# Three stages of a hybrid layer become one: gates, triangular solve and scans, with two pieces of linear attention moved in the order of TensorE

## The reference

```python
# gated delta rule, 4 heads, keys and values of 128
diff = G[..., :, None] - G[..., None, :]                 # G: running sum of the log decay
decay = jnp.where(causal, jnp.exp(jnp.where(causal, diff, 0.0)), 0.0)
lower = jnp.eye(c) + jnp.where(strict, einsum(k_beta, k) * decay, 0.0)
uw = triangular_solve(lower, concatenate([v * beta, k_beta * exp(G)]))
attn = einsum(q, k) * decay
def step(S, chunk):                                       # scan over the chunks
    v_new = u - w @ S
    o = (q * exp(g)) @ S + attn @ v_new
    S = S * exp(g_last) + (k * exp(g_last - g)).T @ v_new
# gated linear attention, 4 heads, keys of 64, values of 128
def step(S, chunk):
    o = (q * exp(b)) @ S + attn @ v
    S = diag(exp(b_last)) @ S + (k * exp(b_last - b)).T @ v
```

## Time and profile before

| what | value |
|---|---|
| median of 3 runs | 2036.91 us (2035.85 to 2037.27) |
| the profiled execution | 2038.26 us, of which 2036.6 us lie between its first and last instruction |
| mean granted TensorE clock | 0.984 |
| PE busy | 1942.1 us, 95% |
| DVE busy | 1173.8 us, 58% |
| ACT busy | 850.5 us, 42% |
| POOL busy | 338.9 us, 17% |

### The profile page before, as it was taken

How to read it: one execution, slowest core, us unless ns; L and a number is a source line. 1 busy time by engine, 2 the same in 40 slices (tenths; PEclk the granted TensorE clock), 3 DMA queues, 4 the chain that set the end, 5 groups by cost and what they waited for, 6 DMA issues and landing times. The chain is left out here.

```text
span 2036.6 us, 26346 instructions
## 1 busy us (share of the span) xinstructions
PE 1942.1 (95%) x10678; PEld 1561.7 (77%) x10678; DVE 1173.8 (58%) x1459; ACT 850.5 (42%) x1212; POOL 338.9 (17%) x276
## 2 busy tenths in 40 slices
PE   8999898999989899898999999999999999999998
PEld 5887876788887688555788888878789878888886
DVE  4655866565676632476577357545654467736752
ACT  4246533435733522464444234333344445413432
POOL 1500614230151400242220000012000021000002
PEclk9999999999989899999999999999999999999999
DMA  6220121222012132201132333224222112232221
GB/s 242 83 74 31 44 84 62 104 83 83 1 44 104 62 104 99 77 1 44 62 122 70 106 104 104 80 96 145 83 83 83 42 42 104 84 113 88 99 85 70
DMA packets 30780, 167.60 MB, mean 82 GB/s; under 512 B 2827, under 2 KB 9635, under 8 KB 14916
## 3 DMA queue, kind: packets, MB, share of 16 engines
q1 hardware_dynamic: 30228, 165.13, 23.4%
q10 hardware_dynamic: 432, 0.79, 0.1%
HBM read 159.58 MB, written 10.00 MB: 83 GB/s over the span
## 5 line engine op out<-in xcount | busy, mean ns | idle before, releaser
L318 PE MATMUL psum<-inputs_high,weights_high 128*128 128x512 f32 x928 | 382.2, 412 | 20.3 <-DVE inputs_low L266 11.9
L319 PE MATMUL psum<-inputs_low,weights_high 128*128 128x512 f32 x928 | 365.0, 393 | 0.0
L320 PE MATMUL psum<-inputs_high,weights_low 128*128 128x512 f32 x928 | 364.5, 393 | 0.0
L2215 PE MATMUL psum<-inputs_high,weights_high 128*128 128x512 f32 x704 | 276.1, 392 | 0.5 <-DVE inputs_low L2359 0.5
L2216 PE MATMUL psum<-inputs_low,weights_high 128*128 128x512 f32 x704 | 274.0, 389 | 0.0
L2217 PE MATMUL psum<-inputs_high,weights_low 128*128 128x512 f32 x704 | 274.0, 389 | 0.0
L271 DVE TENSOR_TENSOR weights_low<-weights_raw,weights_high 128x2048 fp32r<-128x2048 f32 x66 | 155.4, 2355 | 165.3 <-ACT weights_high L260 165.3
L318 PEld LDWEIGHTS psum<-inputs_high,weights_high 128*128 128x128 f32 x928 | 176.5, 190 | 74.8 <-DVE inputs_low L266 14.2
L319 PEld LDWEIGHTS psum<-inputs_low,weights_high 128*128 128x128 f32 x928 | 176.5, 190 | 38.9 <-issue 5.7
L320 PEld LDWEIGHTS psum<-inputs_high,weights_low 128*128 128x128 f32 x928 | 176.0, 190 | 37.9
L2195 ACT CAST weights_high<-weights_raw 128x2048 fp32r<-128x2048 f32 (+1 forms) x72 | 119.5, 1660 | 166.4 <-PE psum L2217 166.4
(11 more groups left out here) (404 smaller groups left out, 3130.2 us busy)
## 6 DMA issues: line engine op xcount, KB each, us to landing
weights_raw<-w_stream SPq DMA_DIRECT2D x116, 1024.0 KB, 4.9
weights_raw<-w_down SPq DMA_DIRECT2D x32, 704.0 KB, 4.1
residual_parked<-residual SPq DMA_DIRECT2D x2, 2048.0 KB, 9.8
residual_back<-residual_parked SPq DMA_DIRECT2D x2, 2048.0 KB, 8.4
residual<-x_t SPq DMA_DIRECT2D x2, 1024.0 KB, 9.8
bias_by_row<-bias_rows SPq DMA_DIRECT2D x2, 1024.0 KB
bias_by_row<-bias_rows SPq DMA_DIRECT2D x1, 1536.0 KB
out_t<-residual SPq DMA_DIRECT2D x5, 256.0 KB, 2.0
```

Of the source, the lines that this page charges most:

```text
L318: pe.matmul(out, hi, self.ahi[:, k], start=start and b == 0, stop=False)
L319: pe.matmul(out, hi, self.alo[:, k], start=False, stop=False)
L320: mm = pe.matmul(out, lo, self.ahi[:, k], start=False, stop=stop and b == blocks - 1)
L2215: pe.matmul(out, wh, hi, start=start, stop=False)
```

## The change

`delta_gates`, `solve` and `scans` no longer make a block each. They return their engines' parts as functions, and a new `recurrences` runs all of them in one block with one set of 41 semaphores, so that each engine goes from one stage to the next when its own waits allow. Waits are added where the block's end had stood: PE's `zero_left` and `turned_read`, ACT's `pair_read` before it clears four banks, DVE's and SP's `scaled`, and PE's wait for the first finished chunk of the last level before the scans. `cleared` keeps ACT from reading a transfer's semaphore before SP has cleared it. SP's two loads of weights (1 MB each) go out once the gates have read the buffer. ACT's part of the weight split moves from the first scan step to the end of the solve.

Linear attention's products of the first chunk (`gla_adds(0)` and both halves of `gla_outputs(0)`, 16 instructions) move from the scans' first step into the solve's first level, on PE between `left` of chunk 1 and of chunk 2. In the scans `gla_adds(1)` and `gla_adds(2)` run one step earlier than before, and the second half of `gla_outputs(t)` runs one step later, between `carried` and `solved`. DVE's wait at the end of a step goes, and one for `gla_out` comes in front of the second half of the state update. The banks of `carried` and `solved`, and the two sets of banks of linear attention, change places.

```diff
+def recurrences(nc, k, layer, h, a, gla, squares):
+    with ExitStack() as stack, phase(nc, "cleared", "row", ..., "gla_early") as s:
+        gates = delta_gates(nc, k, h, a, s, stack)
+        scan = scans(nc, k, h, a, gla, squares, s, stack)
+        inverse = solve(nc, k, layer, h, a, s, scan.linear)
+        with nc.Block() as block:
...
+            @block.tensor
+            def _(pe):
+                gates.tensor(pe)
+                inverse.tensor(pe)
+                scan.tensor(pe)
...
 # solve
+    def sync(sp):
+        sp.sem_inc(s.cleared, 1)
+        sp.wait_ge(s.scaled, 3 * HEADS)
+        sp.wait_ge(s.pair, TT)
         for u in range(2):
             sp.dma_start(k.raw[:, u], ...).then_inc(k.landed[u], 16)
...
         def left(n, t):
+            if n == 0 and t < COUPLED:
+                pe.wait_ge(s.coupled, t + 1)
             if n < mid and 4 * n + t >= COUPLED:
...
+        pe.wait_ge(s.zero_left, 1)
+        pe.wait_ge(s.turned_read, 2 * HEADS)
         for t in range(TT):
             left(0, t)
+            if t == COUPLED - 1:
+                linear(pe)
...
     # scalar, at its end
+        act.wait_ge(s.cleared, 1)
+        act.wait_ge(k.landed[0], 16)
+        act.copy(k.whi[:, 0], k.raw[:, 0]).then_inc(s.high, 1)
...
     # vector, at its start
+        dve.wait_ge(s.scaled, 3 * HEADS)
...
     # gpsimd
                 if n:
                     pool.wait_ge(s.left, 4 * (n - 1) + t + 1)
                     pool.wait_ge(s.inv_t, t + 1)
+                else:
+                    pool.wait_ge(s.pair_read, t + 1)
 # scans
+    def linear(pe):
+        gla_adds(pe, 0)
+        gla_outputs(pe, 0, (0, 1), False)
+        gla_outputs(pe, 0, (2, 3), True)
     def tensor(pe):
+        pe.wait_ge(s.inv_t, TT * (len(LEVELS) - 1) + 1)
         for t in range(TT):
...
                 mm.then_inc(s.carried, 1)
-                if t < end:
-                    gla_adds(t)
+                if t == 1:
+                    pe.wait_ge(s.gla_state, 2)
+                    gla_adds(pe, 2)
+                else:
+                    if t > 2:
+                        pe.wait_ge(s.gla_state, 2 + HEADS * (t - 2))
+                    gla_outputs(pe, t - 1, (2, 3), True)
                 pe.wait_ge(s.rest, t)
...
             mm.then_inc(s.solved, 1)
             if t == 0:
-                gla_adds(t)
+                gla_adds(pe, 1)
             else:
                 pe.wait_ge(s.gla_state, max(2, HEADS * (t - 1)))
-            if t >= 2:
-                pe.wait_ge(s.gla_out_copy, t - 1)
-            gla_outputs(t, (0, 1), False)
+                if t >= 2:
+                    pe.wait_ge(s.gla_out_copy, t - 1)
+                gla_outputs(pe, t, (0, 1), False)
             pe.wait_ge(s.values, t + 1)
...
             mm.then_inc(s.out, 1)
-            if t > 1:
-                pe.wait_ge(s.gla_state, 2 + HEADS * (t - 1))
-            gla_outputs(t, (2, 3), True)
+        pe.wait_ge(s.gla_state, 2 + HEADS * (end - 1))
+        gla_outputs(pe, end, (2, 3), True)
     def vector(dve):
...
             if t > 1:
+                dve.wait_ge(s.gla_out, t)
                 gla_state(t - 1, (2, 3))
...
-            dve.wait_ge(s.gla_out, t + 1)
         rest(end)
+        dve.wait_ge(s.gla_out, end)
         gla_state(end - 1, (2, 3))
```

More of the change, by code:

```diff
@@ L946, in delta_gates @@
     q, kk, v = h.qkv[:, 0:4], h.qkv[:, 4:8], h.qkv[:, 8:12]
[L947 to L1051, removed]
-                row(2)
-                row(3)
-                for n in range(4, 2 * HEADS, 2):
-                    row(n)
-                    row(n + 1)
-                    turn(n // 2)
-                for n in range(HEADS, HEADS + 2):
-                    turn(n)
-                pe.wait_ge(s.kb, HEADS)
-                for n in range(2 * TT):
-                    cols = slice((n % TT) * P, (n % TT + 1) * P)
-                    if n >= 2:
-                        pe.wait_ge(s.pair_read, n - 1)
-                    for hd in range(HEADS):
-                        mm = pe.matmul(ps[:, n % 2, hd * P:(hd + 1) * P], kk[:, hd, cols],
-                                       (kb if n < TT else q)[:, hd, cols], start=True, stop=True)
-                    mm.then_inc(s.pair, 1)
-                    if n in (1, 3):
-                        turn(HEADS + 2 + n // 2)
@@ L1076, in solve @@
+    return named(scalar=scalar, vector=vector, gpsimd=gpsimd, tensor=tensor)
+def solve(nc, k, layer, h, a, s, linear):
     ps, con = k.ps, k.con
@@ new lines, in recurrences @@
+def recurrences(nc, k, layer, h, a, gla, squares):
+    with ExitStack() as stack, phase(
+            nc, "cleared", "row", "row_exp", "diff", "decay", "masked", "kb", "scaled", "turned", "turned_read",
+            "last_arg", "last_exp", "pair", "pair_read", "coupled", "zero_left",
+            "coupling", "left", "left_copy", "both", "inv", "inv_t", "zero_both",
+            "zero", "carried", "rest", "solved", "values", "out", "out_copy", "added", "state", "gla_out", "gla_out_copy",
+            "gla_added", "gla_state", "squared", "high", "split", "gated", "gla_early") as s:
+        gates = delta_gates(nc, k, h, a, s, stack)
+        scan = scans(nc, k, h, a, gla, squares, s, stack)
+        inverse = solve(nc, k, layer, h, a, s, scan.linear)
@@ L1173, in _ @@
-                for t in range(TT):
-                    left(0, t)
-                for m in range(first_step, steps + behind):
-                    if m < steps:
-                        left(m // TT, m % TT)
-                    if m - behind >= first_step:
-                        both((m - behind) // TT, (m - behind) % TT)
+                gates.tensor(pe)
+                inverse.tensor(pe)
+                scan.tensor(pe)
+            @block.vector
+            def _(dve):
+                gates.vector(dve)
+                inverse.vector(dve)
+                scan.vector(dve)
@@ L1233, in _ @@
+                gates.scalar(act)
+                inverse.scalar(act)
+                scan.scalar(act)
             @block.gpsimd
             def _(pool):
[L1235 to L1241 removed]
@@ L1400, in gate_outputs @@
+                gates.gpsimd(pool)
+                inverse.gpsimd(pool)
+                scan.gpsimd(pool)
 def gate_outputs(dve, s, k, h, t, mixers, copied=None):
```

620 lines of the change are left out of this document (365 added, 255 removed).

## The result

The changed kernel takes 2023.5 us in the median (2022.07 to 2026.19, 4 runs) against 2037.09 (2035.85 to 2039.1, 4 runs): a ratio of 0.9935 with a 95% interval of 0.9923 to 0.9947. That is 13.6 us faster, where 6.7 were forecast, and lies outside the range. The profiled execution takes 2023.1 us, of which 2021.3 lie in the span; the span before was 2036.6, so 15.3 us are to be explained.

The account below looks back on a forecast made before the run. POOL's masks were taken to set the solve's pace, PE the scans'. The terms 0.39 + 0.9 + 0.85 + 0.32 + 0.9 give 3.36 us a layer, 6.7 for two: 2030.2 against 2036.91, range 2027 to 2034.

Parts of the forecast that it names:

- Gates to solve: Without the block's end POOL's masks of the solve start earlier and all 18 move: 0.39 us saved a layer.
- Linear attention in the first level: The 16 instructions moved into the solve's first level take 1.79 us on PE, hidden by POOL's masks: no cost.
- Rival 1: Those 16 instructions run at low clock, POOL waits 1.75 us a layer: 2033.7 us, no change; chance 0.09.
- Solve to scans: PE goes from the solve's last products to `solved` of step 0 without the block end's wait: 0.9 us saved a layer.
- first step: Scans' step 0: PE issues 32 instructions instead of 40 between `solved` and `carried`, clock returning as before: 0.85 us saved a layer.
- The bound of 3.5 us: Upper bound of the saving in the scans' step 0, if none of the 32 instructions runs at low clock.
- Step 1: Scans: half of `gla_outputs(1)`, 0.90 us on PE, leaves, but DVE's weight split limits the saving to 0.32 us a layer.
- step 2: Scans: nothing follows `out`, so `carried` of step 3 comes 0.9 us earlier a layer; DVE fits by 0.3.
- Rival 3: DVE becomes the bound of the scans' step 2 as well, 0.9 us a layer lost: 2032.0 us; chance 0.11.
- step 3: Scans: half of `gla_outputs(2)`, 0.9 us, fills the 0.85 in which PE waited for DVE; no change in length.
- SP's later transfer: At the next stage's start SP clears 41 semaphores instead of 19; its first transfer comes 1.2 us later, hidden.
- Rivals 2 and 4: Scans' low clock: returns some 5.3 us later, 2035.5 us, chance 0.08; or stays through the whole scans, 2068, chance 0.03.

Follow-up runs that it names:

- cut_gates: The changed kernel with the block end between gates and solve put back, solve and scans still in one block; 2030.0 us.
- spread: The changed kernel with linear attention's 16 instructions moved from the solve's first level, two into each of the solve's last eight steps; 2027.8 us.
- before_filled: The kernel before with two idle instructions, whose result nobody reads, added in each of the solve's last eight steps; 2034.4 us.
- after: The changed kernel itself, in its first measurement and profile; 2023.5 us against 2037.09 for the kernel before.
- again: The changed kernel, unaltered, measured and profiled once more; 2025.9 us.
- split_early: The changed kernel with DVE's first weight split moved to its idle time at the solve's end, and the clearing of `gst` given to GpSimd; 2024.5 us.
- late_half: The changed kernel with DVE's weight split early, `gst` cleared on GpSimd, and eight of linear attention's 16 instructions in the solve's last steps; 2027.4 us.
- after_later: The changed kernel with DVE's subtraction before the last solved step of the second layer's scans made three times instead of once; 2029.4 us.

## Why the prediction was right in its order and wrong in its time

- **Gates to solve, 0.39.** Right: 0.40 and 0.55 up to the last mask. `cut_gates`, with the block end back, shows 38.55 and 38.66 there.
- **Linear attention in the first level, nothing.** Right: the 16 instructions start 0.112 apart, and POOL shows no idle time. Without POOL's cover they cost 16.11 - 14.20 = 1.9 (`spread` against the first layer of the changed kernel, both at the high clock), near the 1.79 worked out. Rival 1 is out.
- **Solve to scans, 0.9; first step, 0.85.** Right at one clock: 0.85 and 0.77. Wrong in the profile, where both together gave 4.90 and 2.74. The step that failed is the sentence that the clock "comes back as long after the start as before". It stayed up in one layer and came back some 3.3 us after `solved` in the other (588.53 to 591.8), where 4.2 to 5.4 were taken over; so `carried` of step 1 came 3.77 and 5.28 after `solved`, where 6.25 was forecast. The bound of 3.5 us stood in the text for the first step alone, and I placed myself in its middle from two measured ramps that both had the block end in them. For the solve's end the sum priced no change of the clock at all.
- **Step 1, 0.32; step 2, 0.9.** Right: `solved` of step 2 comes 268.71 - 259.76 = 8.95 after `carried` of step 1, where it was 9.25, and `carried` of step 3 comes 4.62 behind it instead of 5.5. DVE's split did become what PE waits for. Rival 3 is out; step 3 changed by 0.06.
- **SP's later transfer.** Right: it is issued 2.3 us after the next stage's first cast, and nothing waits for it.
- **What no term held.** Order and waits come to 0.40 + 0.55 + 2 x (1.61 + 1.19 + 0.06) = 6.7 us, the sum that was forecast. The rest of the 15.3, 8.6 us, is the clock: 4.90 + 2.74 - 2 x 1.61 = 4.4 at the solve's end, and 4.2 in stages that the change doesn't touch. The sum has no term for the stages behind the second layer, and that is the second step that failed. Rivals 2 and 4 looked for a longer low stretch; a shorter one was in the text only as the first step's bound, and no chance was given to it by itself. That order and waits come so near to the forecast sum is no luck, since its terms hold one by one; the time as a whole missed. Single runs agree, as far as the mean granted clock of a run tells: two of the kernel before had 0.989 and took 2031.6 and 2033.3, and four of the changed kernel with 0.989 took 2025.7 to 2027.9, some 6 us less, where the medians lie 11.3 to 13.6 apart.

Shown: filling the solve's end removes the low stretch there, and the block end before the scans goes with a longer one. Why it does is not shown; the rows suggest that the standstill in the low stretch puts off the return of the clock. A standstill of 0.78 us did not bring the clock down by itself: in both layers of `before_filled` it happens at 1.00 and the clock stays. The Trainium skill, TensorE: Matmul & The Clock Gate, section "HAM oscillation — how this bites in real kernels", tells of waits for transfers between groups of products that bring the low clock back. Those waits are longer than 0.78 us, so `before_filled` neither bears that out nor speaks against it.

Not settled: why the later stages take 1405.7 to 1406.4 us in four of the sixteen profiles (after, again, split_early, cut_gates) and 1408.7 to 1410.3 in the other twelve. The clock goes with it: up to the span's end these stages spend 19.8 to 23.0 us at the low clock in the four, 28.4 to 35.9 in the twelve. All four have the new order. The place goes with it too: the first low stretch behind the second layer begins 61.5 to 62.1 us after the next stage's first cast in the four and 59.6 to 60.4 in eleven of the twelve (`late_half`, at 1408.7, has 61.6). With its delay `after_later` went from the first place to the second; the kernel before, delayed, only reached 60.4, so whether the place gives the fast form was not tested. So 4.2 of the 15.3 us in the profile may be lost again to any edit that shifts these stages.

## What to carry to other kernels

Work out the saving at one clock, and then ask separately whether the stretch begins or ends at the low clock, what would lengthen or shorten that, and how much work lies under it: here this second sum was larger than the first. A block end in a stretch at the low clock may cost more than its idle time: here such stretches were 3.4 us longer. Before a gain is credited to an edit, look at the stages that it doesn't touch, and repeat the profile: one execution shows only one of several places where the clock may fall.

## What the runs showed of the hardware that was not expected

The same code at the same place shows low stretches of different length: at the solve's end of the changed order, in `after`, `again` and their two delayed forms, none in three layers and 6.8 us in five, worth 16.5 to 17.0 against 14.0 to 14.2 from mask to carried. The Trainium skill, TensorE: Matmul & The Clock Gate, section "What's actually happening", says of a kernel's start that the number of products at the low clock varies between runs of one kernel; these profiles agree, and show it in the middle of a program. And a delay of 1.43 us in one step cost the changed kernel 3.3 us more in stages tens to hundreds of microseconds later: behind the second layer it spent 28.4 us at the low clock, the changed kernel 19.8.
